# The hybrid decoder trunk on one core: the recurrence's levels in pairs, two to a visit and to a PSUM bank, and two of ScalarE's copies placed later

## Chip, cores and metric

The kernel runs on one core of one Trainium2 chip. The metric is device time in microseconds for one execution of the whole program; the kernel before took 2767.3 us, the median of 3 runs (2766.99 to 2767.32).

TensorE (PE in the rows), VectorE (DVE), ScalarE (ACT) and GpSimd (POOL) each work through a list of their own in order. The list of SyncE (SP) issues the DMAs. Semaphores tie the lists together.

## What is computed

One inference step of a two-layer decoder trunk, for 2048 prompt tokens and 64 sample tokens (8 sequences of 8). Each layer has a projection, two parallel branches (windowed attention and a gated linear recurrence), an output projection with a layer norm, and a gate. The change concerns the recurrence alone. The reference computes it with four heads of 128 x 128 state:

```python
lbf = lb.astype(jnp.float32)
log_f = jnp.logaddexp(jnp.log(lbf), jnp.log1p(-lbf) + jax.nn.log_sigmoid(f_logit.astype(jnp.float32)))
k = -jnp.expm1(log_f)
...
def step(S, blk):
    qc, gc, kc, vc = blk
    G = jnp.cumsum(gc, axis=1)
    diff = G[:, :, None] - G[:, None, :]
    decay = jnp.exp(jnp.where(causal, diff, NEG_INF))
    A = jnp.einsum('bthd,bshd,btshd->bhts', qc, kc, decay)
    o = jnp.einsum('bhts,bshv->bthv', A, vc) + jnp.einsum('bthd,bhdv->bthv', qc * jnp.exp(G), S)
    G_last = G[:, -1]
    S_new = jnp.exp(G_last)[..., None] * S + jnp.einsum(
        'bshd,bshv->bhdv', kc * jnp.exp(G_last[:, None] - G), vc)
    return S_new, o
```

The output o is normed per head, multiplied by a SiLU gate, and goes with the attention's output into the output projection.

## The kernel before

**Phases.** For each of the two layers the program has an attention phase, a recurrence phase (`recurrence_phase`) and an output phase. The recurrence goes over NT = 17 tiles of 128 tokens: tile 0 holds the 64 sample tokens, tiles 1 to 16 the prompt. The order on every engine is written out by hand.

**The matrix A by levels.** Within a tile, A[s, t] for s < t is made in seven levels, h = 64, 32, 16, 8, 4, 2, 1 (`LEVELS`; the text calls them level 0 to level 6), and a diagonal. At level h the tile is cut into blocks of 2h tokens; the second half of each block is multiplied with the first half, both scaled by the exponential of the decay's distance from the middle of the block. The stations of a level are:

1. VectorE, `sub_level` (L1520, L1521): differences of G from the block's middle into `E[l % 2]`. It waits for `level_prod` of two levels before, since E is double buffered.
2. ScalarE, in `middle` (L1366): the exponential of E in place.
3. GpSimd, `level` (L1262): two multiplications, q by E into `qE[l % 2]` and k by E into `kE[l % 2]`, called the factors here. It waits for `level_mm` of two levels before.
4. TensorE, `level` (L1703 for h of 64 and 32, L1707 for the others): 8 or 16 small matmuls with 32 columns of weights into the PSUM bank `LV[l % 2]`. Each shows in the trace as two records.
5. VectorE, `take_level` (L1530, L1538): from the bank into A or into `near`, the 32 x 32 blocks on the diagonal.

**What TensorE does beside it.** In `step(n, k)` TensorE projects the next tile's q, f, g and v (`project`, products at L121 through `split_products`: three per chunk of 128 input rows, 8 chunks, 512 columns each). The levels of tile n are strewn between chunks of that projection: level 0 after chunks 0 and 1 of f, level 1 after 2 and 3, and so on; level 6 stands right before the diagonal (L1715). Between them stand the turning of u (`transpose_u`, L1689, of the tile before) and of q and f of the next tile (`transpose_qf`, L1681 and L1683), which need ScalarE's help: `copy_uT` (L1406) brings u^T out of PSUM for its store by SP, and `copy_z` (L1331) brings q and f out, so that they can be turned. In eight steps of a layer, tiles 3 to 10, `add_sample` (L1750) and `new_dec` (L1615) also update one sample sequence's state, with bank `LV[1]`. A step ends with the turning of kh, the output O and the state's update in M (L1723, L1733, L1734, L1739).

**ScalarE's order in a step.** `middle` does the seven exponentials. `copy_uT` follows the fourth (`if l == (6 if ... else 3)`), then `copy_z(n + 1)` (`if l == 3` in `after`); `split_high` of the next input follows the second. Behind the seventh come the exponentials of the ends (L1377 to L1380), for which GpSimd waits, and then `front_log`, which needs the next tile's g (`z_g`) and starts the next tile's decay.

**The last tile.** While tile 16 goes through its levels, TensorE already does the first products of the output phase (`lead.mix(pe, n, c)`: block n, chunk c, six products). `mix` waits for the low part of the weights' chunk, which VectorE makes (`following.remainder`, L215), one chunk after each `sub_level`; ScalarE rounds the chunks between its exponentials. In step 15, ScalarE and GpSimd split the two blocks of mixT (`lead.split_high`, L313, and `lead.split_low`, L318), which SP loads behind `store_mix`.

## Time and profile before

| | before |
| --- | --- |
| median of 3 runs | 2767.3 us |
| profiled execution | 2765.99 us |
| its span | 2764.2 us, granted clock 0.98 |
| TensorE busy | 2668.4 us, 97% |
| VectorE busy | 1511.1 us, 55% |
| ScalarE busy | 1048.3 us, 38% |
| GpSimd busy | 1044.2 us, 38% |
| recurrence's steps, layer 0 | from about 440 to about 907 us |
| recurrence's steps, layer 1 | end at about 2289 us |

The span is the time between the first and the last instruction of the profiled execution. Matmuls overlap in the trace, so the start of one to the start of the next is what one costs, not its duration. In the chain of waits the pieces follow each other without overlap, so they can be added.

### The profile page before, as it was taken

The page shows a single profiled execution, that of the slowest core. Times are in us where ns is not written, and L with a number is a line of the kernel's source. Part 1 is how long each engine was busy: PE and PEld are TensorE (multiplying, and loading weights), DVE is VectorE, ACT ScalarE, POOL GpSimd, SP SyncE. Part 2 cuts the span into 40 slices and gives each one's busy share as a digit, 9 for nine tenths or more (in the row PEclk, how much of TensorE's full clock was granted, in tenths as well). Part 3 has the DMA queues.
Part 4 walks back from the last instruction along what each step waited for, and adds up shares of the span by engine and source line. Part 5 has one row for each costly group of instructions (what it writes and reads, how often), then busy time and mean ns, then how long its engine had stood idle before and what let it go on. Part 6 is the DMA issues. An engine that isn't in the chain of part 4 may idle for free.

```text
span 2764.2 us, 54510 instructions
## 1 busy us (share of the span) xinstructions
PE 2668.4 (97%) x21010; PEld 2152.0 (78%) x21010; DVE 1511.1 (55%) x3052; ACT 1048.3 (38%) x2305; POOL 1044.2 (38%) x959
## 2 busy tenths in 40 slices
PE   7999989999999799999989999899999997999998
PEld 6777768788877678888777777687888776788887
DVE  5566665677766732222336666656777667322222
ACT  3333354555555521111233333545555555111111
POOL 2222214555555533233212222145555555333332
PEclk9999999999999899999999999989999998999999
...
DMA packets 103450, 190.75 MB, mean 69 GB/s; under 512 B 11744, under 2 KB 64992, under 8 KB 101216
## 3 DMA queue, kind: packets, MB, share of 16 engines
...
q8 instruction: 112, 1.84, 0.3%
q14 instruction: 42, 0.34, 0.0%
q10 hardware_dynamic: 432, 0.08, 0.0%
...
## 4 chain that ended last, share of the span: by engine, by line
PE 90%; issue 3%; DVE 2%; POOL 2%; ACT 1%; DMA 1%; SPq 1%; DVEq 0%; POOLq 0%; ACTq 0%
PE r_Z L121 25%; PE a_Z L121 16%; PE o_GT L2142 13%; PE o_MX L2142 12%; PE o_PL L2142 3%; PE r_LV L1707 2%; PE a_T L977 2%; PE a_SC L956 2%; PE r_LV L1703 1%; PE o_HT L2166 1%; PE a_SC L966 1%; PE r_O L1733 1%; PE r_M L1739 1%; PE r_O L1734 1%; PE o_MX L121 1%
## 5 line engine op out<-in xcount | busy, mean ns | idle before, releaser
L121 PE MATMUL r_Z<-w_rec_high,w_rec_xh 128*128 128x512 f32 x1024 | 433.3, 423 | 1.5 <-DVE r_kT L1484 0.9
L121 PE MATMUL r_Z<-w_rec_high,w_rec_xl 128*128 128x512 f32 x1024 | 403.4, 394 | 0.0
L121 PE MATMUL r_Z<-w_rec_low,w_rec_xh 128*128 128x512 f32 x1024 | 402.7, 393 | 0.0
L121 PE MATMUL a_Z<-w_attn_high,w_attn_xh 128*128 128x512 f32 (+1 forms) x816 | 304.8, 374 | 15.3 <-DVE w_attn_low L213 12.9
L121 PE MATMUL a_Z<-w_attn_high,w_attn_xl 128*128 128x512 f32 (+1 forms) x816 | 292.2, 358 | 0.0
L121 PE MATMUL a_Z<-w_attn_low,w_attn_xh 128*128 128x512 f32 (+1 forms) x816 | 292.0, 358 | 0.0
L1262 POOL TENSOR_TENSOR r_qE<-r_qT,r_E 128x256 f32<-128x256 f32 x230 | 190.5, 828 | 265.4 <-ACT r_E L1366 249.6
L1366 ACT ACTIVATE r_E<-r_E 128x512 f32<-128x512 f32 x230 | 141.5, 630 | 250.3 <-DVE r_E L1521 250.3
L121 PEld LDWEIGHTS r_Z<-w_rec_high,w_rec_xl 128*128 128x128 f32 x1024 | 193.6, 189 | 43.2
L121 PEld LDWEIGHTS r_Z<-w_rec_high,w_rec_xh 128*128 128x128 f32 x1024 | 193.5, 189 | 42.0 <-issue 2.9
L121 PEld LDWEIGHTS r_Z<-w_rec_low,w_rec_xh 128*128 128x128 f32 x1024 | 194.3, 190 | 30.6
L2142 PE MATMUL o_GT<-w_out_high,o_hh 128*128 128x512 f32 x512 | 202.6, 396 | 5.9 <-issue 5.9
L1520 DVE TENSOR_TENSOR r_E<-r_G 128x256 f32<-128x256 f32 x230 | 141.8, 617 | 113.1 <-POOL r_kE L1262 98.2
L2097 DVE SCALAR_TENSOR_TENSOR o_th<-o_th,o_PL 128x1024 f32<-128x1024 f32 x34 | 41.5, 1222 | 296.3 <-PE o_PL L2142 296.3
L2142 PE MATMUL o_MX<-w_out_high,o_mh 128*128 128x512 f32 x480 | 191.4, 399 | 11.4 <-POOL o_ml L1944 11.4
L2142 PE MATMUL o_GT<-w_out_high,o_hl 128*128 128x512 f32 x512 | 201.1, 393 | 0.0
L2142 PE MATMUL o_GT<-w_out_low,o_hh 128*128 128x512 f32 x512 | 201.0, 393 | 0.0
L1262 POOL TENSOR_TENSOR r_kE<-r_kT,r_E 128x256 f32<-128x256 f32 x230 | 200.2, 870 | 0.0
L121 PEld LDWEIGHTS a_Z<-w_attn_high,w_attn_xh 128*128 128x128 f32 x816 | 156.2, 191 | 43.3 <-issue 21.2
L2142 PE MATMUL o_MX<-w_out_low,o_mh 128*128 128x512 f32 x480 | 188.6, 393 | 0.0
L2142 PE MATMUL o_MX<-w_out_high,o_ml 128*128 128x512 f32 x480 | 188.5, 393 | 0.0
L2010 ACT ACTIVATE o_th<-o_GT 128x1024 f32<-128x1024 f32 x34 | 35.0, 1029 | 396.5 <-PE o_GT L2142 376.0
...
## 6 DMA issues: line engine op xcount, KB each, us to landing
...
```

Of the source, the lines that this page charges most:

```text
L121: mm = pe.matmul(out, a[:, c, :], b[:, c, :], start=(first and c == chunks[0] and a is xh and b is wh), stop=(last and c == chunks[-1] and ...
L956: mm = pe.matmul(scores[r:r + 64, 4 * s + i, r:r + 192], qT[rows, i, r:r + 64], keys[:, first_key + r:first_key + r + 192], start=True, st ...
L966: t = pe.transpose(turned[:, h, :], probs[:, h, :], C["ident"][:, :])
L977: mm = pe.matmul(T[d, :], v[tile][:, d], pT[:, i, 4 * s:4 * s + 4, :].rearrange("p h t -> p (h t)"), start=(i == 0), stop=(i == 1))
L1262: op = pool.tensor_tensor(to, halves(flat(q_or_k), h)[half], halves(E[i][:, :], h)[half], ALU.mult)
L1366: act.activation(E[l % 2][:, :], E[l % 2][:, :], ACT.Exp).then_inc(S["level_exp"].sem, 1)
L1520: dve.tensor_tensor(to1, mid, first, ALU.subtract)
L1703: mm = pe.matmul(LV[i][r:r + NEAR, g * h:g * h + h], kE[i][:, g * P + r:g * P + r + NEAR], qE[i][:, g, q], start=True, stop=True)
L1707: mm = pe.matmul(LV[i][r:r + NEAR, g * 16:g * 16 + 16], kE[i][:, g * P + r:g * P + r + NEAR], qE[i][:, g, r // 2:r // 2 + 16], start=True, ...
L2010: act.activation(th[:, :], GT[:, :], ACT.Tanh, scale=0.5).then_inc(S["tanh_done"].sem, 1)
L2097: dve.scalar_tensor_tensor(out=th[:, :], in0=th[:, :], scalar=1.0, in1=PL[:, :], op0=ALU.add, op1=ALU.mult).then_inc(S["blend"].sem, 1)
L2142: mm = pe.matmul(out[0][:, out[1]], a[:, c, :], w, start=(c == 0 and a is high and b is wh), stop=(c == chunks - 1 and a is low))
```

## The change

**Pairs.** Levels 2p and 2p + 1 now go into one bank, `LV[p % 2]`, side by side: the odd one starts at column 256 (`level_bank`). TensorE does both without a projection product between them, and waits for `level_took` only ahead of the even one. So a step has the visits (0, 1), (2, 3), (4, 5) and 6 with the diagonal, where before it had 0, 1, 2, 3, 4, 5 and 6 with the diagonal. The chunks of the projection are dealt out anew between them.

**VectorE** takes two levels after the differences of the odd level that follows: 0 and 1 after those of level 3, 2 and 3 after those of level 5; 4, 5 and 6 after the kh differences. It waits for the products of the whole pair (`visited`). In tile 1, `gated(0, ...)` moves from after level 4 to after level 5.

**ScalarE** does `copy_uT(n - 1)` and `copy_z(n + 1)` behind the sixth exponential (l = 5), no longer behind the fourth. In step 15 the second `lead.split_high` moves from behind the fifth to behind the seventh.

**The last tile**: `lead.mix(pe, 0, 0)` comes ahead of level 0, and the mixes are dealt out in fours between the pairs. In tile 0, the turning of q and f comes ahead of level 0.

The core of the diff:

```diff
@@ -1160,6 +1160,10 @@
         def tokens(n):
 
             return DEC if first(n) else P
+
+        def level_bank(l):
+
+            return LV[l // 2 % 2][:, l % 2 * 256:l % 2 * 256 + 256]
 
         def passed(n):
 
@@ -1364,7 +1368,7 @@
                 for l, h in enumerate(levels):
                     act.wait_ge(*S["level_sub"].at(passed(n) + l + 1))
                     act.activation(E[l % 2][:, :], E[l % 2][:, :], ACT.Exp).then_inc(S["level_exp"].sem, 1)
-                    if l == (6 if isinstance(n, int) and n == 1 else 3):
+                    if l == (6 if isinstance(n, int) and n == 1 else 5):
                         copy_uT(n - 1)
                     after(l)
                 act.wait_ge(*S["khx_done"].at(n + 1))
@@ -1434,13 +1438,13 @@
                 def after(l):
                     if l == 1 and last:
                         lead.split_high(act, 0)
-                    elif l == 4 and last:
+                    elif l == 6 and last:
                         lead.split_high(act, 1)
                     elif l == 1:
                         split_high(n + 2, k)
                     if l == 2 and isinstance(n, int) and n == 1:
                         squares(0, M, DEC)
-                    if l == 3:
+                    if l == 5:
                         copy_z(n + 1)
 
                 middle(n, LEVELS, after)
@@ -1520,12 +1524,12 @@
                 dve.tensor_tensor(to1, mid, first, ALU.subtract)
                 dve.tensor_tensor(to2, second, mid, ALU.subtract).then_inc(S["level_sub"].sem, 1)
 
-            def take_level(n, l, h):
-
-
-                src = LV[l % 2]
+            def take_level(n, l, h, visited):
+
+
+                src = level_bank(l)
                 if h >= NEAR:
-                    dve.wait_ge(*S["level_mm"].at(passed(n) + l + 1))
+                    dve.wait_ge(*S["level_mm"].at(passed(n) + visited))
                     for r in range(0, P, 2 * h):
                         op = dve.tensor_copy(A[r:r + h, :, r + h:r + 2 * h],
                                              src[r:r + h, 0:GH * h].rearrange("p (g t) -> p g t", g=GH))
@@ -1534,7 +1538,7 @@
                         .unsqueeze(1).to_broadcast([P, GH, NEAR // (2 * h), h])
                     if l:
                         dve.wait_ge(*S["level_took"].at(passed(n) + l))
-                    wait_apart(dve, S["dve_passed"], S["level_mm"], passed(n) + l + 1)
+                    wait_apart(dve, S["dve_passed"], S["level_mm"], passed(n) + visited)
                     op = dve.copy_predicated(near[:, :, :].rearrange("p g (n s t) -> p g n s t", s=2, t=h)[:, :, :, 1, :], mask,
                                              src[:, 0:GH * NEAR // 2].rearrange("p (g n t) -> p g n t", g=GH, t=h))
                 op.then_inc(S["level_took"].sem, 1)
@@ -1551,12 +1555,13 @@
                 dve.wait_ge(*S["sum_done"].at(n + 1))
                 if sample is not None:
                     sample_rows(sample)
+                NLEV = len(levels)
                 for l, h in enumerate(levels):
                     sub_level(n, l, h)
                     after(l)
                     if l == 0 and not first(n):
                         silu(n, k)
-                    if l == 4 and second:
+                    if l == 5 and second:
                         gated(0, 0, M, DEC)
                     elif l == 1 and not first(n) and not second:
                         new_state(n - 1)
@@ -1567,8 +1572,9 @@
                         dve.wait_ge(*S["oT_ps"].at(1))
                     elif l == 0:
                         wait(dve, S["o_done"], n)
-                    if l >= 2:
-                        take_level(n, l - 2, levels[l - 2])
+                    if l >= 3 and l % 2:
+                        for taken in (l - 3, l - 2):
+                            take_level(n, taken, levels[taken], l - 1)
                 if first(n):
                     g8 = G[:, :, 0:DEC].rearrange("p g (b t) -> p g b t", t=DEC_SEQ)
                     for g in range(GH):
@@ -1581,8 +1587,8 @@
                     wait(dve, S["khT_ps"], n)
                     dve.tensor_tensor(kh[:, :, :], G[:, :, P - 1:P].to_broadcast([P, GH, P]), G[:, :, :],
                                       ALU.subtract).then_inc(S["khx_done"].sem, 1)
-                for l in (len(levels) - 2, len(levels) - 1):
-                    take_level(n, l, levels[l])
+                for l in range(NLEV - 3 if NLEV > 3 else 0, NLEV):
+                    take_level(n, l, levels[l], min(l // 2 * 2 + 2, NLEV))
                 take_near(n, levels)
 
             def new_state(n):
@@ -1690,21 +1696,22 @@
                 t.then_inc(S["uT_ps"].sem, 1)
 
             def level(n, l, h, sample=None):
-                i, at = l % 2, passed(n) + l
+                i, at, to = l % 2, passed(n) + l, level_bank(l)
                 if sample is not None:
                     pe.wait_ge(*S["sd_done"].at(sample + 1))
                 pe.wait_ge(*S["level_prod"].at(at + 1))
-                wait(pe, S["level_took"], at - (1 if l else 0))
+                if l % 2 == 0:
+                    wait(pe, S["level_took"], at - (2 if l else 0))
                 for g in range(GH):
                     if h >= NEAR:
                         for r in range(0, P, NEAR):
                             block, q = r // (2 * h), slice(r // (2 * h) * h, r // (2 * h) * h + h)
                             if r % (2 * h) < h:
-                                mm = pe.matmul(LV[i][r:r + NEAR, g * h:g * h + h],
+                                mm = pe.matmul(to[r:r + NEAR, g * h:g * h + h],
                                                kE[i][:, g * P + r:g * P + r + NEAR], qE[i][:, g, q], start=True, stop=True)
                     else:
                         for r in range(0, P, NEAR):
-                            mm = pe.matmul(LV[i][r:r + NEAR, g * 16:g * 16 + 16], kE[i][:, g * P + r:g * P + r + NEAR],
+                            mm = pe.matmul(to[r:r + NEAR, g * 16:g * 16 + 16], kE[i][:, g * P + r:g * P + r + NEAR],
                                            qE[i][:, g, r // 2:r // 2 + 16], start=True, stop=True)
                 mm.then_inc(S["level_mm"].sem, 1)
 
@@ -1758,28 +1765,27 @@
                     add_sample(n, sample)
                 if second:
                     turn_samples()
-                project(*later, "f", 0, 2)
+                project(*later, "f", 0, 4)
                 level(n, 0, LEVELS[0])
-                project(*later, "f", 2, 4)
-                level(n, 1, LEVELS[1], sample)
-                project(*later, "f", 4, 6)
+                level(n, 1, LEVELS[1])
+                project(*later, "f", 4, KC)
+                project(*later, "g", 0, 2)
                 if not second:
                     transpose_u(n - 1)
-                level(n, 2, LEVELS[2])
-                project(*later, "f", 6, KC)
+                level(n, 2, LEVELS[2], sample)
                 level(n, 3, LEVELS[3])
-                project(*later, "g", 0, 2)
+                project(*later, "g", 2, 4)
                 transpose_qf(n + 1)
-                project(*later, "g", 2, 4)
-                level(n, 4, LEVELS[4])
                 project(*later, "g", 4, 6)
                 if second:
                     transpose_u(0)
+                level(n, 4, LEVELS[4])
                 level(n, 5, LEVELS[5])
                 project(*later, "g", 6, KC)
+                project(*later, "v", 0, 2)
                 level(n, 6, LEVELS[6])
                 diagonal(n)
-                project(*later, "v")
+                project(*later, "v", 2, KC)
                 transpose_kh(n)
                 if second:
                     pe.wait_ge(*S["zeroed"].at(2))
@@ -1810,11 +1816,10 @@
 
             for what in "qfg":
                 project(1, 1, what)
+            transpose_qf(1)
             level(0, 0, DEC_LEVELS[0])
-            transpose_qf(1)
-            project(1, 1, "v", 0, 2)
             level(0, 1, DEC_LEVELS[1])
-            project(1, 1, "v", 2, 4)
+            project(1, 1, "v", 0, 4)
             level(0, 2, DEC_LEVELS[2])
             diagonal(0)
             project(1, 1, "v", 4, 6)
@@ -1837,19 +1842,24 @@
                 step(2 * j, 0)
             n = NT - 1
             step(n - 1, 1)
-            level(n, 0, LEVELS[0])
             pe.wait_ge(*S["qT_sb"].at(NT))
             pe.wait_ge(*S["kx_done"].at(NT))
             lead.mix(pe, 0, 0)
+            level(n, 0, LEVELS[0])
             level(n, 1, LEVELS[1])
             transpose_u(n - 1)
             pe.wait_ge(*S["gate_done"].at(NT))
             pe.wait_ge(*S["v_copied"].at(NT))
             lead.mix(pe, 1, 0)
-            for l in range(2, NL):
-                lead.mix(pe, 0, l - 1)
+            lead.mix(pe, 0, 1)
+            lead.mix(pe, 1, 1)
+            for l in (2, 4):
                 level(n, l, LEVELS[l])
-                lead.mix(pe, 1, l - 1)
+                level(n, l + 1, LEVELS[l + 1])
+                for c in (l, l + 1):
+                    lead.mix(pe, 0, c)
+                    lead.mix(pe, 1, c)
+            level(n, 6, LEVELS[6])
             diagonal(n)
             lead.mix(pe, 0, NL - 1)
             transpose_kh(n)
```

**What stands where.** TensorE in a step of layer 0, from the turning of u on; r0_qE0 and r0_qE1 are the two factor buffers, even and odd levels. Before:

```order
L1689 MATMUL r0_M<-ident,r0_u 128x128 x4
L1707 MATMUL r0_LV0<-r0_qE0,r0_kE0 32x16 x16
L121 MATMUL r0_Z<-w_rec_high,w_rec_xh1 128x512
L121 MATMUL r0_Z<-w_rec_low,w_rec_xh1 128x512
L121 MATMUL r0_Z<-w_rec_high,w_rec_xl1 128x512
...
L1707 MATMUL r0_LV1<-r0_qE1,r0_kE1 32x16 x16
```

In the changed kernel, from the same point to the turning of q and f:

```order
L1695 MATMUL r0_M<-ident,r0_u 128x128 x4
L1714 MATMUL r0_LV1<-r0_qE0,r0_kE0 32x16 x16
L1714 MATMUL r0_LV1<-r0_qE1,r0_kE1 32x16 x16
L121 MATMUL r0_Z<-w_rec_high,w_rec_xh1 128x512
L121 MATMUL r0_Z<-w_rec_low,w_rec_xh1 128x512
L121 MATMUL r0_Z<-w_rec_high,w_rec_xl1 128x512
...
L1687 MATMUL r0_Z<-ident,r0_zqf 128x128 x4
L1689 MATMUL r0_Z<-ident,r0_zqf 128x128 x4
```

Levels 2 and 3 stand together, in bank LV1, and the six projection products that parted them now stand behind both.

ScalarE in the same kind of step, from the third exponential to the exponentials of the ends (E0 and E1 are the even and odd levels' buffers; zqf is the copy of q and f, r0_u<-r0_M that of u^T). Before:

```order
L1366 ACTIVATE r0_E0<-r0_E0 128x512
L1366 ACTIVATE r0_E1<-r0_E1 128x512
L1406 ACTIVATE r0_u<-r0_M 128x512
L1331 ACTIVATE r0_zqf<-r0_Z 128x1024
L1366 ACTIVATE r0_E0<-r0_E0 128x512
L1366 ACTIVATE r0_E1<-r0_E1 128x512
L1366 ACTIVATE r0_E0<-r0_E0 128x512
L1377 ACTIVATE r0_decay<-r0_G 128x4
L1379 ACTIVATE r0_kh<-r0_kh 128x512
L1380 ACTIVATE r0_qG<-r0_G 128x512
```

In the changed kernel:

```order
L1370 ACTIVATE r0_E0<-r0_E0 128x512
L1370 ACTIVATE r0_E1<-r0_E1 128x512
L1370 ACTIVATE r0_E0<-r0_E0 128x512
L1370 ACTIVATE r0_E1<-r0_E1 128x512
L1410 ACTIVATE r0_u<-r0_M 128x512
L1335 ACTIVATE r0_zqf<-r0_Z 128x1024
L1370 ACTIVATE r0_E0<-r0_E0 128x512
L1381 ACTIVATE r0_decay<-r0_G 128x4
L1383 ACTIVATE r0_kh<-r0_kh 128x512
L1384 ACTIVATE r0_qG<-r0_G 128x512
```

The two copies moved behind two more exponentials, so that six stand ahead of them and one behind.

TensorE at the start of the last tile, from the state's update on (o0_MX and o0_HT take the mix of blocks 0 and 1). Before:

```order
L1739 MATMUL r0_M<-r0_v,r0_khT 128x128 x4
L1703 MATMUL r0_LV0<-r0_qE0,r0_kE0 32x64 x8
L121 MATMUL o0_MX<-w_out_high0,o0_mh0 128x512
L121 MATMUL o0_MX<-w_out_low0,o0_mh0 128x512
L121 MATMUL o0_MX<-w_out_high0,o0_ml0 128x512
...
L1703 MATMUL r0_LV1<-r0_qE1,r0_kE1 32x32 x8
L1689 MATMUL r0_M<-ident,r0_u 128x128 x4
L121 MATMUL o0_HT<-w_out_high0,w_rec_xh1 128x512
```

In the changed kernel:

```order
L1746 MATMUL r0_M<-r0_v,r0_khT 128x128 x4
L121 MATMUL o0_MX<-w_out_high0,o0_mh0 128x512
L121 MATMUL o0_MX<-w_out_low0,o0_mh0 128x512
L121 MATMUL o0_MX<-w_out_high0,o0_ml0 128x512
...
L1710 MATMUL r0_LV0<-r0_qE0,r0_kE0 32x64 x8
L1710 MATMUL r0_LV0<-r0_qE1,r0_kE1 32x32 x8
L1695 MATMUL r0_M<-ident,r0_u 128x128 x4
L121 MATMUL o0_HT<-w_out_high0,w_rec_xh1 128x512
```

The first mix products moved ahead of level 0, and levels 0 and 1 stand together.

## Rows read from the trace of the kernel before

**Rows 1.** The page, chain that ended last: shares of the span by engine.

```profile
PE 90%; issue 3%; DVE 2%; POOL 2%; ACT 1%; DMA 1%; SPq 1%; DVEq 0%; POOLq 0%; ACTq 0%
```

**Rows 2.** Chain in order of time, one step: start us, us, what.

```profile
813.59 6.83 PE r_Z L121 x30
820.42 0.57 PE r_LV L1703 x16
820.99 1.58 PE r_Z L121 x6
...
828.90 0.44 PE r_Z L1681 x4
```

**Rows 3.** Timeline of PE, two visits: start us, us, instruction, xcount.

```profile
580.44 0.39 PE L121 MATMUL r_Z<-w_rec_high,w_rec_xl 128*128 128x512 f32 x1
580.75 0.45 PE L1707 MATMUL r_LV<-r_qE,r_kE 128*32 128x16 f32 x32
581.13 0.50 PE L121 MATMUL r_Z<-w_rec_high,w_rec_xh 128*128 128x512 f32 x1
581.47 0.39 PE L121 MATMUL r_Z<-w_rec_low,w_rec_xh 128*128 128x512 f32 x1
...
582.39 0.40 PE L121 MATMUL r_Z<-w_rec_high,w_rec_xl 128*128 128x512 f32 x1
582.72 0.45 PE L1707 MATMUL r_LV<-r_qE,r_kE 128*32 128x16 f32 x32
582.99 0.47 PE L1715 MATMUL r_M<-r_qT,r_kT 128*32 128x32 f32 x32
...
583.74 0.40 PE L121 MATMUL r_Z<-w_rec_low,w_rec_xh 128*128 128x512 f32 x1
```

**Rows 4.** Timelines of DVE, ACT and POOL in the step from 813.59; idle in brackets.

```profile
825.48 0.95 DVE L1521 TENSOR_TENSOR r_E<-r_G 128x256 f32<-128x256 f32 x1
...
826.93 0.42 DVE L1521 TENSOR_TENSOR r_E<-r_G 128x256 f32<-128x256 f32 x1
...
825.00 0.60 ACT L1406 ACTIVATE r_u<-r_M 128x512 f32<-128x512 f32 x1 [1.06 <-PE r_M L1689]
...
826.98 1.03 ACT L1331 ACTIVATE r_zqf<-r_Z 128x1024 f32<-128x1024 f32 x1 [1.38 <-PE r_Z L121]
...
827.90 1.14 ACT L1366 ACTIVATE r_E<-r_E 128x512 f32<-128x512 f32 x2
...
825.22 0.93 POOL L1262 TENSOR_TENSOR r_kE<-r_kT,r_E 128x256 f32<-128x256 f32 x1
```

**Rows 5.** Chain in order of time, a step with a sample's update.

```profile
560.37 5.49 PE r_Z L121 x24
565.86 0.89 PE r_LV L1750 x8
```

**Rows 6.** Timeline of DVE in that step.

```profile
573.45 0.95 DVE L1521 TENSOR_TENSOR r_E<-r_G 128x256 f32<-128x256 f32 x1
```

**Rows 7.** Timelines in tile 0, in step 15 and in the last tile.

```profile
411.13 0.21 DVE L1538 COPY_PREDICATED r_near<-near,r_LV 128x64 f32<-128x64 int32 x1
...
911.21 1.29 DVE L215 SCALAR_TENSOR_TENSOR w_out_low<-w_out_whole,gains,w_out_high 128x1024 fp32r<-128x1024 f32 x1 [0.70 <-ACT w_out_high L203]
...
891.97 1.06 ACT L313 ACTIVATE w_rec_xh<-w_rec_raw 128x1024 fp32r<-128x1024 f32 x1 [1.52 <-DMA w_rec_raw<-dram_mixT]
...
918.06 0.73 POOL L1262 TENSOR_TENSOR r_kE<-r_kT,r_E 128x256 f32<-128x256 f32 x1
...
895.78 0.44 PE L1707 MATMUL r_LV<-r_qE,r_kE 128*32 128x16 f32 x32 [0.75 <-POOL r_kE L1262]
...
916.48 1.07 PE L1703 MATMUL r_LV<-r_qE,r_kE 128*32 128x64 f32 x16 [9.20 <-POOL r_kE L1262]
```

**Rows 8.** Windows: stretch, length, busy time of each engine, PEclk, DMA share, GB/s.

```profile
916.00:918.00 2.00, 1.52 (x17) 1.33 (x18) 2.00 (x4) 1.54 (x2) 1.84 (x2) 0.50 1.05 410
922.00:924.00 2.00, 2.00 (x11) 1.58 (x9) 2.00 (x4) 0.71 (x2) 1.22 (x2) 1.00 0.03 8
```

## The prediction

> **What bounds the kernel now.** I read the shares of the chain that ended last first [rows 1]: 90% of the span is TensorE work, and no other engine or queue holds more than 2%. Then the chain in order of time through one step of the recurrence, the one that starts at 813.59 [rows 2]: there it is TensorE alone, piece after piece with nothing between, so in a step every nanosecond that TensorE saves is saved, as long as nobody makes it wait. There are 15 such steps in each of the two layers, 30 in all. Below, "+x" is the time after a step's start. Last I read TensorE's own timeline around two visits to the levels [rows 3]. Projection products of 512 columns start every 0.23 us (581.47 to 582.39 are four). The sixth level's visit (580.75) costs more than its own products: from the projection product at 580.44 to the one at 581.47 there are 1.03 us where two products take 0.46, so a visit costs 0.57. Of that about 0.08 goes on entering (0.31 instead of 0.23 to the first small product) and 0.11 on the product after the return (0.34 instead of 0.23), the rest is the 0.38 of the visit, whose last 0.11 is a tail: in the next visit the level's products hand over to those of the diagonal after 0.27 (582.72 to 582.99).
>
> **Two levels a visit.** That next visit is the experiment that I need, already in the trace: level 6 and diagonal side by side. From 582.39 to 583.74 are 1.35, less 0.46 is 0.89, so the second set of small products added 0.32 where a visit of its own costs 0.57. It has 32 columns; a level of 16 columns should add only the 0.27 until handover. So a merge saves 0.25 at least and 0.30 if the handover row holds for it; an upper bound is 0.32 (entry 0.10 as at 582.39 to 582.72, tail 0.11, return 0.11). I take 0.30, since the second sets in this change are levels, which is the row for the same shapes. A step goes from seven visits to four (levels 0 and 1; 2 and 3; 4 and 5; 6 with the diagonal as now), so three merges: 0.90 a step, 27.0 over 30 steps, bounds 22.5 and 28.8. The number of products, their shapes and banks' total use stay as they are.
>
> What the rows show is that leaving the wide products for the 32-column ones and coming back costs some 0.2 to 0.3 us each time. The Trainium skill, TensorEngine Tiling, Key Properties, says that changing the tiling mode drains TensorE, while changing only the tile doesn't; by that rule the saving is the whole price of a switch, and it holds for level 0 with its 64 columns too. The trace bears it out for level 6 and the diagonal; no row here shows it for two levels.
>
> **What the waits of the merged visits cost.** A merged visit needs the factors of both levels. Level 0's visit now starts at +6.83 [rows 2] and moves behind two more chunks of f: 6 products, 1.38, so +8.2. Then come both levels (0.57 - 0.11 + 0.38 = 0.84), 18 projection products (the six right after a visit take 1.58, the other twelve 2.77) and the turning of u (as long as that of q at 828.90, 0.44): levels 2 and 3 at about +13.9. GpSimd's factors of level 3 end at 825.22 + 0.93, +12.6 [rows 4], and nothing ahead of them moves later: 1.3 to spare. So this wait costs nothing. The last pair has what it needs earlier still, because ScalarE no longer stops between the exponentials: now it waits 1.38 there for f (826.98 in [rows 4]).
>
> **What is moved behind the third pair, and where it is tight.** TensorE turns q and f (now at 828.90, +15.3) right after two chunks of g. By the sum above that comes to +13.9 + 0.65 + 1.6 = +16.1. It needs ScalarE's copy of q and f, and that copy now stands behind the sixth exponential and the copy of u^T. The chain to it [rows 4]: VectorE's differences for level 4 end at 825.48 + 0.95, +12.8. Those for level 5 need the factors of level 3 (+12.6), so they follow at once; if GpSimd stands still meanwhile they take 0.76, as the pair that ends with 826.93 does: +13.6. And it does stand still, for its factors of level 4 need level 2's product, at +14.2 or later. Then the exponential of level 5 (0.57), the copy of u^T (0.60, of which ScalarE overlaps about 0.1 with the next) and the copy of q and f (1.03): about +15.7. That leaves 0.3 us, and the copy of u^T finds its input, turned at +13.4 to +13.9, just ready. The eight steps of a layer that also update a sample's state have less. Such a step starts at 560.37 and has 0.89 more on TensorE before level 0 [rows 5], which puts the turn of q and f at +17.0. The differences of level 4 end at 573.45 + 0.95, which is +14.0 [rows 6], so the copy ends at about +16.9. There it is a tie, and I take 0.1 for 15 or so of the 30 steps: 1.5 lost. Bounds: none lost, or 0.2 in each step, 6.0. SP's store of u^T and the load behind it move later by some 2.7 us. They have over 10 us until the next gated u needs the buffer, so no price.
>
> **The edges.** (a) In tile 0, VectorE no longer takes a level (0.21, 411.13 in [rows 7]) ahead of the differences that ScalarE's chain waits for: 0.15 a layer, 0.3. (b) In step 15 of each layer ScalarE splits the second block of mixT; now it waits for its load, 1.52, in layer 0 (891.97 in [rows 7]), and TensorE with it. That load is queued on SP behind the store of u^T, which moves later, and the split moves behind the seventh exponential, with the exponentials of the ends and the logarithm for the last tile queued behind it on ScalarE. I put 0.9 on this wait. In layer 0 it takes the place of the 0.75 that TensorE loses now (row 895.78), so it costs nothing there; in layer 1, where little is lost now, it costs 0.9. Bounds: 0 and 2.4 (0.9 + 1.52). (c) In the last tile TensorE waits 9.20 us for GpSimd (916.48 in [rows 7]); after it the clock is at half [rows 8], and the first six mix products run at it, 2.8 us by twice the spacing of [rows 3]. They need only chunk 0's low part, which VectorE has at 911.21 + 1.29. The change puts them first, so they go into the wait. But level 1 must wait until 918.06 + 0.73 for its factors, and from there VectorE's splitting of the weights paces the levels. I take a gain of 0.4 a layer, 0.8; bounds are a gain of 1.1 each and a loss of 2.1 each (below).
>
> **The sum.** 27.0 - 1.5 + 0.3 - 0.9 + 0.8 = 25.7. The profiled execution took 2765.99 us (span 2764.2), which gives 2740.3. It stands 1.3 under the median of the three runs shown, 2767.3, and against that I forecast 2741.6.
>
> **The rivals.** First, the clock in the last tile. Its granted clock is 0.50 in 916 to 918 and back at 1.00 by 922 to 924, after unbroken work from 916.48 [rows 8]. Changed, TensorE works on six products from 912.5, stops, does level 0, stops for level 1 and again for u. If these stops keep it at 1.2 GHz, the next 18 mix products take 8.3 instead of 4.1 us. They start about 1.1 earlier than now, and a wait of about 1 for level 3's factors hides some of it: about 2.1 lost per layer instead of 0.4 gained, some 5 us over both, 2746.6. The Trainium skill, TensorE: Matmul & The Clock Gate, Why this matters for your kernels, asks for continuous work before the full clock comes back, and so speaks against this part of the change; rows 8 agree that unbroken work brings it back. Chance 0.09.
>
> Second, the merges save nothing: the price would lie in each level's own hand-over and not in the switch. Then only the edges remain and the tie at q and f costs 1.5: 2767 to 2769. The visit with the diagonal in [rows 3] speaks against it. Chance 0.04. Third, the copy of q and f comes late by a full 1.1 in every step, because VectorE's level-5 differences run while GpSimd works: 0.95 and more for each instead of 0.42, as the row at 825.48 has it beside 825.22. That gives back the 0.90, about 2766. What speaks against it is that GpSimd must wait for level 2's product. Chance 0.04. The Trainium skill, SBUF — State Buffer, section SBUF: two separate sides, calls the shared port an exclusive lock for the whole instruction; the rows show both sides stretched, 0.95 and 0.93, which is the same direction.
>
> Fourth, and slower: the same place, but with level 4's differences late as well, since level 2's factors wait for a level-0 product that is now 1.4 later (+8.2). Then the two delays of 1.1 add up, the turn of q and f stalls about 2.0 beyond its slack, and each step is 1.1 longer: 33 us, 2800. It decides when the copy of q and f ends more than 1.2 us after the +15.7 worked out. Against it: level 2's exponential ends at about +9.4, after level 0's product even when moved. Chance 0.03. That the change doesn't do what it says I don't hold a case of its own: the order has the levels in pairs in all 30 steps.
>
> **How the numbers follow.** Forecast 2741.6, chance 0.80, own range 2735 to 2751. The range for 8 in 10 takes in the bounds: all at their best 28.8 + 0.3 + 2.2 = 31.3, 2736, with 2 us for what one execution leaves open, 2734; and on the other side 22.5 - 6.0 + 0.3 - 0.9 - 2 = 13.9, 2753.4, so 2754. The clock rival lies in it. A difference of 0.2% (5.5 us) is about what a measurement of this kernel can tell from none. Faster by more than that: the forecast and the first rival, 0.89. Within it: the second and third, 0.08. Slower: 0.03.
>
> **What would show it.** In the changed profile a step without a sample should take 30.0 to 30.1 us on TensorE, with about 0.27 from the first to the second set of a pair and 0.38 for the second. TensorE should wait nowhere but, if anywhere, for ScalarE's copy of q and f, 0.1 at most. The factors of level 3 should end 1 us or more before their visit, and the two differences of level 5 should take about 0.42 each. ScalarE should have no wait for f between its exponentials. In the last tile the first mix products should start at about 912.5 less what was saved before, with the clock as above. I am wrong if a wait for q and f of 0.5 or more stands in most steps, if a pair costs what two visits did, or if the last tile grows by more than 2 us.

## The result and the profile after

The changed kernel takes 2739.86 us (median of 4 runs, 2738.89 to 2740.91); the kernel before took 2767.31 in the same comparison. The ratio is 0.9906, with a 95% interval of 0.9893 to 0.992: 27.45 us, or 1.0%, faster. The profiled execution took 2740.13 us (span 2738.3), 25.86 less than that of before. The forecast was 2741.6.

The page of the changed kernel has TensorE's busy time 24.0 us lower than before, and the shares of the chain that ended last, beside [rows 1], are still nearly all TensorE:

```profile
PE 2644.4 (97%) x21010; PEld 2158.7 (79%) x21010; DVE 1514.6 (55%) x3052; ACT 1048.6 (38%) x2305; POOL 1038.6 (38%) x959
```

```profile
PE 90%; DVE 3%; ACT 2%; issue 2%; DMA 1%; POOL 1%; SPq 1%; DVEq 0%; POOLq 0%; ACTq 0%
```

The chain of waits through one step without a sample, in the place of [rows 2] (start us, us, what):

```profile
770.39 8.19 PE r_Z L121 x36
778.57 0.81 PE r_LV L1710 x29
779.39 4.31 PE r_Z L121 x18
783.70 0.44 PE r_M L1695 x4
784.13 0.67 PE r_LV L1714 x52
784.80 1.59 PE r_Z L121 x6
786.39 0.44 PE r_Z L1687 x4
...
788.67 0.67 PE r_LV L1714 x52
789.34 2.94 PE r_Z L121 x12
792.28 0.38 PE r_LV L1714 x32
...
800.40 0.69 PE r_Z L121 x3
```

Nothing stands between TensorE's pieces. The step takes 800.40 - 770.39 = 30.01 us. A pair of levels costs 0.67 (with level 0 in it 0.81), where two visits to levels of 16 columns cost 0.38 each and 0.20 more for the return to the wide products after each (1.59 for six of them instead of 1.38 to 1.41).

The rest of the comparison is one table. It is worked out from VectorE's timeline: the time from its first product of kT in one tile (L1484 before, L1488 after) to the same in the next. That cuts the recurrence into stretches of one tile each, in layer 0 / layer 1. The last row goes from there to the last update product of tile 16 (L1739 before, L1746 after). "Before, again" is the first experiment below.

| stretch | before | before, again | after | gained | forecast |
| --- | --- | --- | --- | --- | --- |
| tile 0 | 20.18 / 20.18 | 20.18 / 20.18 | 20.03 / 20.04 | 0.29 | 0.3 |
| tile 1 | 43.30 / 44.95 | 46.54 / 46.59 | 42.83 / 46.04 | -0.62 | 1.8 |
| steps 2 to 14 | 409.97 / 409.89 | 410.14 / 409.92 | 397.69 / 397.57 | 24.60 | 21.9 |
| step 15 | 31.68 / 30.85 | 31.74 / 32.00 | 29.97 / 30.74 | 1.82 | 0.9 |
| last tile | 42.67 / 42.76 | 42.94 / 42.87 | 42.00 / 43.34 | 0.09 | 0.8 |
| outside the recurrence | | | | -0.32 | 0 |
| sum | | | | 25.86 | 25.7 |

The total fits better than its parts do, and the rows of tile 1 and of the last tile, from one execution each, are mostly chance, as the experiments show. The 1.5 us that the forecast took off for the tie at the copy of q and f are counted with steps 2 to 14.

### The profile page after: what moved, and what is told of

Read it like the earlier page. It is cut to its first block, busy times and chain, and to the rows that moved or that the text cites. A ratio compares the mean times of both kernels' runs of the same rounds, so it can differ in the third digit from the quotient of the medians.

```text
span 2738.3 us, 54412 instructions
## 1 busy us (share of the span) xinstructions
PE 2644.4 (97%) x21010; PEld 2158.7 (79%) x21010; DVE 1514.6 (55%) x3052; ACT 1048.6 (38%) x2305; POOL 1038.6 (38%) x959
## 4 chain that ended last, share of the span: by engine, by line
PE 90%; DVE 3%; ACT 2%; issue 2%; DMA 1%; POOL 1%; SPq 1%; DVEq 0%; POOLq 0%; ACTq 0%
PE r_Z L121 25%; PE a_Z L121 16%; PE o_GT L2152 13%; PE o_MX L2152 12%; PE o_PL L2152 3%; PE a_T L977 2%; PE r_LV L1714 2%; PE a_SC L956 2%; PE o_HT L2176 1%; PE r_M L1746 1%; PE r_O L1741 1%; PE r_O L1740 1%; PE a_SC L966 1%; PE r_Z L259 1%; PE r_LV L1710 1%
## 5 line engine op out<-in xcount | busy, mean ns | idle before, releaser
L121 PE MATMUL r_Z<-w_rec_high,w_rec_xh 128*128 128x512 f32 x1024 | 423.4, 414 | 1.5 <-DVE r_kT L1488 0.9
L121 PEld LDWEIGHTS r_Z<-w_rec_high,w_rec_xl 128*128 128x128 f32 x1024 | 193.8, 189 | 42.7
L121 PEld LDWEIGHTS r_Z<-w_rec_high,w_rec_xh 128*128 128x128 f32 x1024 | 193.9, 189 | 41.2 <-issue 2.9
L121 PEld LDWEIGHTS a_Z<-w_attn_high,w_attn_xl 128*128 128x128 f32 x816 | 155.6, 191 | 23.9
```

Of the source, the lines that this page charges most:

```text
L121: mm = pe.matmul(out, a[:, c, :], b[:, c, :], start=(first and c == chunks[0] and a is xh and b is wh), stop=(last and c == chunks[-1] and ...
```

## The experiments

**The kernel before, once more.** No edit.

> The kernel before, once more, as it is. Between the two traces shown, stretches that the change doesn't touch differ too: 0.8 us in the attention of layer 1 and 2.5 us between the layers. If those are chance from one execution to the next, this trace moves by as much against the first trace of before in the same places; if the change causes them in a way not seen, it reproduces the first trace within 0.3 us there. Its steps should take 30.95 us and, with a sample, 31.89 in either case.

Measured: 2772.7 us. Its steps take 30.95 to 30.99 us and 31.86 to 31.90 with a sample, as before. But tile 1 takes 46.54 and 46.59 us where the first trace has 43.30 and 44.95, and step 15 of layer 1 takes 32.00 instead of 30.85. So these two stretches change by up to 3.3 and 1.2 us with no change at all, and the rows "tile 1" and "step 15" of the table, read alone, say nothing on the change. Outside the recurrence it moves too. The first product of kT in layer 0 starts at 396.44 instead of 397.22 (the changed kernel: 395.04), and from layer 0's last update product to the first kT of layer 1 it has 834.4 us instead of 833.6. The changed kernel has 836.0 there, which is more than this one run shows; but the other kernels of this study, with the same code in that place, have 833.0 to 835.4.

**One merge undone.** In `step`:

```diff
                 level(n, 4, LEVELS[4])
-                level(n, 5, LEVELS[5])
                 project(*later, "g", 6, KC)
+                level(n, 5, LEVELS[5])
                 project(*later, "v", 0, 2)
```

> The changed kernel with one merge undone: level 5 stands two chunks of g behind level 4, everything else stays. Theory: each merge saves the price of leaving the wide products and coming back, 0.31 us, so a step without a sample takes 30.33 us instead of 30.02, a sample step 31.29 instead of 30.98, and 30 steps cost 9.3 us: 2749.2. Rival, the gain lies in ScalarE's order and the merges only fill the time: a step stays at 30.02 and the total at 2740.

Measured: 2745.43 us (2744.09 to 2747.24), ratio to before 0.993 (0.9911 to 0.9949). Steps take 30.30 us and 31.21 with a sample; steps 2 to 14 take 401.24 in each layer where the changed kernel has 397.63 on average: 3.61 / 13 = 0.28 for each merge. Its chain shows where (start us, us, what):

```profile
789.47 0.38 PE r_LV L1714 x32
789.85 1.59 PE r_Z L121 x6
791.43 0.38 PE r_LV L1714 x32
791.81 1.59 PE r_Z L121 x6
```

These 3.94 us stand where the changed kernel has 0.67 + 2.94 = 3.61, and the six products ahead take 0.04 less. The price lies in the merge, and ScalarE's order, which is the same in both, doesn't supply it. The total is 5.6 us over the changed kernel's, not the 9.3 expected and not the 8.4 that 30 steps at 0.28 make: tile 1 takes 40.92 and 45.75 us in this trace, 2.2 less than in that of the changed kernel. So the price is read from the steps, which agree from one to the next, and not from the total.

**All three merges undone**, with the banks, the waits, VectorE's takes and ScalarE's copies left as the change has them:

```diff
                 level(n, 0, LEVELS[0])
+                project(*later, "f", 4, 6)
                 level(n, 1, LEVELS[1])
-                project(*later, "f", 4, KC)
+                project(*later, "f", 6, KC)
...
                 level(n, 2, LEVELS[2], sample)
-                level(n, 3, LEVELS[3])
                 project(*later, "g", 2, 4)
+                level(n, 3, LEVELS[3])
```

(and level 5 as above.)

> The changed kernel with all three merges of a step undone (level 1 behind chunks 4 and 5 of f, level 3 behind chunks 2 and 3 of g, level 5 behind chunks 6 and 7 of g); ScalarE's copies, the banks and VectorE's takes stay as in the changed kernel. Theory: three times 0.31, a step takes 30.95 us, as before the change, and the total is 2740 + 28 = 2768. Rival, part of the gain is ScalarE's no longer stopping between the exponentials or the fewer waits of VectorE: a step stays well under 30.95, by as much as that part is worth, and the total is under 2760.

Measured: 2763.58 us (2760.12 to 2767.49 in 10 runs), ratio 0.999 (0.9979 to 1.0001), so no longer to be told from before. Steps take 30.91 and 31.83 us, steps 2 to 14 409.29 in each layer: (409.29 - 397.63) / 13 = 0.90 for the three merges. A step gained 0.946, so this kernel keeps 0.05 over the one before. A likely place, argued and not tested, is level 3, which stands here right ahead of the turning of q and f: TensorE returns to wide work there at a price of 0.59 - 0.44 = 0.15 instead of 0.20. In the changed kernel no level stands there, so if this is the place, undoing the merges gives back 0.05 less than they are worth, and the whole 0.946 is theirs. By the pieces of the two chains, levels 0 and 1 give 0.36, levels 2 and 3 0.23 with that 0.05 missing, levels 4 and 5 0.31.

```profile
799.27 0.38 PE r_LV L1714 x32
799.65 0.59 PE r_Z L1687 x4
```

**The diagonal parted from level 6**, a set of 32-column products that isn't a level:

```diff
+                diagonal(n)
                 project(*later, "v", 0, 2)
                 level(n, 6, LEVELS[6])
-                diagonal(n)
```

> The changed kernel with the opposite of a merge where before already had one: the diagonal's 32-column products stand two chunks of v ahead of level 6 instead of right behind it; the last tile stays as it is. Theory, the price belongs to the switch, whatever set of 32-column products is parted: 0.31 us a step, 30.33 without a sample, 30 steps cost 9.3 us, total 2749. Rival, the price belongs to a level's own hand-over (its wait on GpSimd's factors and its bank), which the diagonal doesn't have: under 0.1 us a step, total 2740 to 2743.

Measured: 2743.73 us (2743.32 to 2747.95), ratio 0.9921 (0.9902 to 0.9939). Steps take 30.26 to 30.32 us, steps 2 to 14 401.14: 3.51 / 13 = 0.27 a step. The total is only 3.9 us over the changed kernel's, where the steps say 8.1 and 9.3 was expected; the reading rests on the steps again. The chain (start us, us, what):

```profile
798.61 0.39 PE r_M L1722 x32
799.00 1.59 PE r_Z L121 x6
800.59 0.38 PE r_LV L1714 x32
```

The diagonal alone costs 0.39 plus 0.2 on the products behind it, like a level. So the price is that of leaving the wide products and coming back, for both kinds of 32-column products that this kernel has. That refutes the rival "a level's own hand-over", in a place that the change doesn't touch. The Trainium skill (TensorEngine Tiling, Key Properties) says that TensorE drains when the tiling mode changes and not when the tile alone does. This case agrees: an excursion costs 0.27 to 0.30 us, and a second set of 32-column products beside the first doesn't pay it again. That it is a drain, no row shows.

**ScalarE's copies back behind the second pair**, all else as changed:

```diff
-                    if l == (6 if isinstance(n, int) and n == 1 else 5):
+                    if l == (6 if isinstance(n, int) and n == 1 else 3):
                         copy_uT(n - 1)
...
-                    if l == 5:
+                    if l == 3:
                         copy_z(n + 1)
```

> The changed kernel with ScalarE's two copies (u^T, then q and f) behind the second pair's exponentials again, as before the change. Theory, the move is what lets the merged visit of levels 4 and 5 find its factors: both exponentials of that pair then wait until the copies are done, about 2.5 us later than the 783.12 of the changed trace, GpSimd's factors of level 5 are ready at +18.8 instead of +17.5, and the visit, due at +18.28, waits 0.5 to 0.6 us in every step: a step takes 30.5 to 30.6 us, 30 steps cost 15 to 18 us, total 2755 to 2758. Rival, the move isn't needed, since the factors had slack: a step stays at 30.02. Rival, the whole gain is the move: a step takes 30.95.

Measured: 2754.88 us (2750.74 to 2759.07), ratio 0.9959 (0.9946 to 0.9972). Steps take 30.65 to 30.68 us, a little over the 30.5 to 30.6 expected: 0.64 more than changed, 16.6 over the 26 steps 2 to 14. Timelines of this kernel, PE in one step, ACT and POOL in the next, 30.66 later (idle before, and for whom, in brackets):

```profile
799.18 0.45 PE L1714 MATMUL r_LV<-r_qE,r_kE 128*32 128x16 f32 x32
800.12 0.45 PE L1714 MATMUL r_LV<-r_qE,r_kE 128*32 128x16 f32 x32 [0.50 <-POOL r_kE L1266]
...
825.41 0.60 ACT L1410 ACTIVATE r_u<-r_M 128x512 f32<-128x512 f32 x1 [3.75 <-PE r_M L1695]
825.90 1.02 ACT L1335 ACTIVATE r_zqf<-r_Z 128x1024 f32<-128x1024 f32 x1
826.81 1.15 ACT L1370 ACTIVATE r_E<-r_E 128x512 f32<-128x512 f32 x2
...
829.71 1.02 POOL L1266 TENSOR_TENSOR r_kE<-r_kT,r_E 128x256 f32<-128x256 f32 x1
```

ScalarE stands 3.75 us for the turned u, the third pair's exponentials come behind the copies, and level 5's factors end at 830.73, when level 4's product has already been done: TensorE stands 0.50 us between the two levels of one visit. Without the move of the copies two thirds of what the merges save is lost.

**The copies moved in the kernel before**, without merges:

```diff
-                    if l == (6 if isinstance(n, int) and n == 1 else 3):
+                    if l == (6 if isinstance(n, int) and n == 1 else 5):
                         copy_uT(n - 1)
...
-                    elif l == 4 and last:
+                    elif l == 6 and last:
...
-                    if l == 3:
+                    if l == 5:
                         copy_z(n + 1)
```

> The kernel before with ScalarE's two copies moved behind the third pair's exponentials and nothing merged (the split of the second mixT block in step 15 stands behind the seventh exponential, as in the change). Theory: nothing is gained, and the turn of q and f, which stands earlier there than in the changed order (+15.3 instead of +16.0), waits 0.2 to 0.4 us for the copy: a step takes 31.2 to 31.3, total 2773 to 2779. Rival, the gain of the change is the move: a step takes 30.0 to 30.5.

Measured: 2785.46 us (2781.93 to 2792.89), ratio 1.008 (1.0055 to 1.0104): slower, and twice as much as expected. A step takes 31.50 us, with a sample 32.18 or 32.96. Timelines of PE, one step without and one with a sample, and of ACT ahead of the first:

```profile
802.05 0.40 PE L121 MATMUL r_Z<-w_rec_high,w_rec_xl 128*128 128x512 f32 x1
802.77 0.66 PE L1681 MATMUL r_Z<-ident,r_zqf 128*128 128x128 f32 x4 [0.33 <-ACT r_zqf L1331]
803.27 0.60 PE L1683 MATMUL r_Z<-ident,r_zqf 128*128 128x128 f32 x4
...
544.20 0.66 PE L1681 MATMUL r_Z<-ident,r_zqf 128*128 128x128 f32 x4 [0.82 <-ACT r_zqf L1331]
...
801.71 1.02 ACT L1331 ACTIVATE r_zqf<-r_Z 128x1024 f32<-128x1024 f32 x1
```

The wait of 0.33 is what the expectation had, and the step loses 0.55. The rest is how idle time is counted. A projection product takes 0.40 in the trace, but without a stop the turning starts 0.23 after it; the idle time is counted only from its end, so it leaves out the first 0.16. From start to start, the turning of q comes 0.72 after the last product instead of 0.23 (0.49 lost), and that of f 0.50 after it instead of 0.44 (0.06 lost): 0.55 together. In the same way a sample step with the wait of 0.82 loses 1.04. The sample steps of 32.18 lose 0.29, with the turning 0.2 us late and no idle time shown at all.

So each half of the change needs the other: merged without the move, two thirds of the gain go into a wait at levels 4 and 5; moved without the merges, a wait at the turning of q and f makes it slower.

**Level 0 first in the last tile**, all else as changed:

```diff
             step(n - 1, 1)
+            level(n, 0, LEVELS[0])
             pe.wait_ge(*S["qT_sb"].at(NT))
             pe.wait_ge(*S["kx_done"].at(NT))
             lead.mix(pe, 0, 0)
-            level(n, 0, LEVELS[0])
             level(n, 1, LEVELS[1])
```

> The changed kernel with level 0 of the last tile ahead of the first six mix products again, as before the change. From VectorE's first write of kT for the last tile to the last tile's update products the changed trace has 42.0 us in layer 0 and 43.3 in layer 1, the two traces of before 42.7 to 42.9 in both. Theory, the six products in the wait are worth 0.4 to 0.7 a layer and the 1.3 between the layers is when the clock comes back: 42.5 to 42.9 in at least one layer, none under 42.3. Rival, the stops after the six products are what keeps the clock at half in layer 1: with level 0 first both layers take 42.0 or less.

Measured: 2737.82 us in one run. The last tile takes 42.55 us in layer 0 and 41.97 in layer 1, 84.5 together, where the changed kernel has 42.00 + 43.34 = 85.3. Neither expectation holds: one layer is over 42.3, the other under it. With one execution of each, 0.8 us is no verdict. The traces with one or all merges undone, the diagonal parted and the sample states spread have the last tile as the changed kernel has it, so there are ten such tiles: 42.00 to 43.39 us, 42.5 on average, beside 42.7 to 42.9 (42.8 on average) in the four of before. The two of this kernel lie among them. What can be read is the clock. In layer 1 of the changed kernel, TensorE stops three times after the six products, and the clock is still at half in 2278 to 2280; in this kernel it works unbroken from 2270.31, and the clock is back in the window from 2274 to 2276. Timeline of PE and windows (stretch, length, busy time of each engine, PEclk, DMA share, GB/s), first changed, then this one:

```profile
2272.07 1.07 PE L1710 MATMUL r_LV<-r_qE,r_kE 128*32 128x64 f32 x16 [0.97 <-POOL r_kE L1266]
2274.41 0.64 PE L1710 MATMUL r_LV<-r_qE,r_kE 128*32 128x32 f32 x16 [1.27 <-POOL r_kE L1266]
2275.51 1.11 PE L1695 MATMUL r_M<-ident,r_u 128*128 128x128 f32 x4 [0.46 <-DVE r_u L1609]
```

```profile
2278.00:2280.00 2.00, 2.00 (x6) 1.52 (x6) 2.00 (x3) 0.89 (x2) 0.97 (x2) 0.50 0.00 0
```

```profile
2270.31 1.06 PE L1710 MATMUL r_LV<-r_qE,r_kE 128*32 128x64 f32 x16 [9.74 <-POOL r_kE L1266]
```

```profile
2274.00:2276.00 2.00, 2.00 (x25) 1.65 (x25) 2.00 (x4) 1.60 (x2) 0.89 (x1) 0.82 0.06 25
```

**Two moves at the edge.** In the changed kernel GpSimd has its factors of level 0 in the last tile only after a root and a split of 3.37 us, all of them behind step 15's output (timeline of POOL, layer 1), though it had stood idle before:

```profile
2266.91 3.37 POOL L318 TENSOR_TENSOR w_rec_xl<-w_rec_raw,w_rec_xh 128x1024 fp32r<-128x1024 f32 x1
2270.24 0.91 POOL L1266 TENSOR_TENSOR r_qE<-r_qT,r_E 128x256 f32<-128x256 f32 x1
```

```diff
-            root(NT - 2)
             lead.split_low(pool, 1)
+            root(NT - 2)
...
-                    elif l == 6 and last:
-                        lead.split_high(act, 1)
...
                 copy_khT(n)
+                if last:
+                    lead.split_high(act, 1)
                 front_exp(n + 1)
```

> The changed kernel with two moves at its edge. (1) In step 15 ScalarE splits the second mixT block behind its copy of kh^T, where it stands idle, instead of behind the seventh exponential. Theory, what step 15 takes over a plain step (30.74 instead of 30.02 in layer 1 of the changed trace, 31.6 and 31.7 in others) is ScalarE waiting for that block's load: 30.1 us at most in both layers, whenever the load comes. Rival, it is a load's contention or the clock: 30.7 stays. (2) GpSimd takes the low part of that block before the root of the last but one tile, where it is idle for 7 us, instead of behind it, so its factors of level 0 in the last tile start 3.0 us earlier. Theory: the last tile is 1 to 2 us shorter a layer; rival, VectorE's splitting of the weights sets the pace there: under 0.5 us.

Measured: 2731.58 us (2730.24 to 2733.5), ratio 0.9874 (0.9855 to 0.9893). Step 15 takes 29.92 us in both layers, and 29.90 or 29.92 in all the traces below with this move, so what it took over a plain step was ScalarE's wait for the block's load. The other move can't have done it: GpSimd starts that split at 2258.77, when step 15 has ended at 2254.72. The last tile takes 40.86 and 40.14 us, 1.1 and 3.2 less than changed; the eight tiles with both moves average 40.4, 2.1 under the ten without, where 1 to 2 was expected. Layer 1 of this kernel (timelines of POOL and PE):

```profile
2258.77 2.35 POOL L318 TENSOR_TENSOR w_rec_xl<-w_rec_raw,w_rec_xh 128x1024 fp32r<-128x1024 f32 x1 [3.75 <-ACT w_rec_xh L313]
...
2264.76 0.89 POOL L1266 TENSOR_TENSOR r_qE<-r_qT,r_E 128x256 f32<-128x256 f32 x1 [1.20 <-ACT r_E L1370]
...
2269.39 0.64 PE L1710 MATMUL r_LV<-r_qE,r_kE 128*32 128x32 f32 x16 [0.28 <-POOL r_kE L1266]
```

**Wide products among the sample states' narrow ones.** Tile 1 was left, with its 41 to 46.6 us from one execution to the next. Its clock is at half for 10 to 21 us in all around the 64 products of 8 columns by which tile 0 reads the sample states.

```diff
-            sample_states(0, 4)
+            sample_states(0, 1)
             project(1, 1, "v", 6, KC)
-            sample_states(4, DEC_BATCH)
+            for b in range(1, DEC_BATCH - 1):
+                sample_states(b, b + 1)
+                project(2, 0, "q", b - 1, b)
+            sample_states(DEC_BATCH - 1, DEC_BATCH)
...
-                project(*later, "q")
+                project(*later, "q", DEC_BATCH - 2 if second else 0)
```

> The changed kernel with tile 2's projection of q, which stood behind the sample states' products, one chunk behind each of six of them (three wide products each), chunks 6 and 7 of v behind the first state; the amount of work is the same. It tests why tile 1 takes 41 to 46.6 us from one execution to the next whatever the kernel: its granted clock is at half for 14 to 20 us after the 64 products of 8 columns. Theory, those narrow products take the clock down, and wide ones among them hold it up: tile 1 takes under 40 us and the total is 2730 or less. Rival, the clock falls for another reason (the wait at the end of tile 0, the heavy work before it): tile 1 stays at 41 to 47 and the total at 2740 plus or minus 4.

Measured: 2738.61 us, with the widest range of all, 2725.51 to 2746.44. In the profiled execution tile 1 takes 49.15 and 49.13 us, outside what either side of the expectation had: here the wide products among the narrow ones didn't hold the clock, so the theory fails as a rule. But this execution is the slowest of the four. That of 2725.51 is 20.9 us faster, with a mean granted clock of 0.985 instead of 0.978; by these two means it spent some 39 us less at half clock, an estimate, which is worth those 20 us. If that was in tile 1, it took about 39 us there, as the theory had it; it has no trace. In the trace the granted clock is down from before 418 to after 444 (windows), through all eight states:

```profile
416.00:418.00 2.00, 2.00 (x15) 1.82 (x14) 1.97 (x9) 0.00 (x0) 0.00 (x0) 0.90 0.00 0
418.00:420.00 2.00, 2.00 (x9) 1.71 (x7) 0.68 (x1) 1.25 (x3) 0.00 (x0) 0.50 0.44 131
...
444.00:446.00 2.00, 2.00 (x9) 1.59 (x8) 0.64 (x2) 2.00 (x10) 0.00 (x0) 0.78 0.00 0
```

**The narrow products bunched**, on top of the two edge moves:

```diff
             transpose_kh(0)
+            project(1, 1, "v", 6, KC)
...
-            sample_states(0, 4)
-            project(1, 1, "v", 6, KC)
-            sample_states(4, DEC_BATCH)
+            sample_states(0, DEC_BATCH)
```

> The kernel with both edge moves (step 15's split and GpSimd's low part) and one more: chunks 6 and 7 of v, which stood between the fourth and the fifth sample state, go ahead of the first one, into the wait for ScalarE's gather, so that all 64 products of 8 columns follow each other and unbroken wide work begins behind them. Parting them with wide products made tile 1 longer (49.1 us, 27 us at half clock), so the theory is now that the clock comes back only when wide work runs unbroken: tile 1 takes 39 to 43 us in both layers instead of 41 to 46.6, total 2724 to 2731. Rival, where the clock falls is chance and the order of the narrow products is nothing to it: tile 1 stays at 41 to 46.6 and the total at 2731 plus or minus 3. A third way: the states' loads come late without the wide products between, a wait of 1 to 3 us a layer in front of the fifth state.

Measured: 2727.06 us (2724.92 to 2728.38), ratio 0.9857 (0.9836 to 0.9879); tile 1 takes 41.00 and 42.19 us. As this kernel and the one with only the edge moves ran on different chips, both were run again side by side:

> The kernel with the two edge moves once more, on the same chip as the next one, since the two were timed on different chips and tile 1's time changes from one execution to the next. If the bunching is worth something, this one keeps tile 1 at 41 to 46.6 us and a total of 2729 to 2734, 2 us or more above the next. If it isn't, both have the same tile 1 and totals within 2 us.

> The kernel with the two edge moves and the sample states' products bunched, once more, beside the one without the bunching. If wide work that runs unbroken brings the clock back sooner: tile 1 at 40 to 43 us in both layers, total 2724 to 2729. If the first look was chance: tile 1 over 43 in one layer at least, total 2729 to 2734.

Measured: 2730.44 us (2728.41 to 2732.05) without the bunching, tile 1 46.05 and 41.23; 2724.36 (2722.4 to 2725.3) with it, ratio to before 0.9844 (0.9827 to 0.986), tile 1 40.76 and 40.66. All four bunched tiles lie between 40.66 and 42.19 (41.2 on average). Eight tiles of kernels that have tile 1 as changed lie between 41.23 and 46.06 (44.0 on average), and the eight in which only step 1's merges, copies or diagonal differ between 40.92 and 46.04. So the bunching takes away the long tiles and leaves the shortest about as short as they were. The bunched kernel's chain and windows:

```profile
417.82 2.79 DMA r_s_dec<-dram_state
...
420.65 6.49 PE r_O L1800 x32
...
427.43 7.67 PE r_Z L121 x24
```

```profile
420.00:422.00 2.00, 1.82 (x14) 1.71 (x13) 1.79 (x5) 1.18 (x3) 0.00 (x0) 0.84 0.91 269
...
430.00:432.00 2.00, 2.00 (x7) 1.53 (x7) 1.61 (x2) 0.17 (x1) 1.92 (x3) 0.60 0.00 0
```

The clock still falls, in the window from 420 to 422, and is back in that from 430 to 432; in the kernel with only the edge moves it comes back in that from 436 to 438 (0.63). The chain now goes through the load of the fifth state, the third way of the expectation; what TensorE loses by it is small, a wait of 0.18 to 0.30 us in the four bunched tiles.

The edit does two things at once. The six products of v also fill a wait for ScalarE's gather (rows of PE, the changed kernel and the bunched one):

```profile
415.55 1.08 PE L1830 MATMUL r_O<-r_A,r_v_dec 128*128 128x64 f32 x8 [0.67 <-ACT r_A L1390]
...
415.94 1.00 PE L1831 MATMUL r_O<-r_A,r_v_dec 128*128 128x64 f32 x8
```

How much each is worth follows from the time at half clock, four times what PEclk lacks to 1 summed over windows of 2 us. It is 10 to 20.5 us in the eight tiles with tile 1 as changed (16.2 on average) and 10.2 to 13.6 in the bunched ones (11.1). Take half of it off, and what is left of the tile is 35.9 us on average and 35.6. So of the 2.9 us that a bunched tile saves, some 2.6 are clock and 0.3 the filled wait (estimates from these windows). What is not shown is the reason that the expectation gave. In layer 1 of the kernel with only the edge moves (41.23 us) the clock is back, at 0.86 and 0.99, in the windows from 1792 to 1796, with the second half of the narrow products in them, and at half again in that from 1796 to 1798: it came back without the long unbroken work behind the last state. The bunched kernel is the fastest of the study, 42 us (1.6%) under the kernel before on the same chip.

## Why the prediction was right, point by point

**The merges.** Forecast: 0.30 for each, 0.90 a step, from the visit of level 6 with the diagonal [rows 3]. Measured by undoing them: 0.90 for the three, 0.28 for levels 4 and 5, 0.27 for level 6 and the diagonal. With the 0.05 that the undone kernel keeps, they may be worth 0.95. The second set of a pair was to start after 0.27 and take 0.38; a pair's 0.67 in the chain is near the sum. The step was to take 30.0 to 30.1 us and takes 30.01.

**The waits of the merged visits.** Levels 2 and 3 were due at +13.9 and come at +13.74. Level 3's factors were due at +12.6 and end at +12.4. Both are in these rows of the step from 770.39 (timelines of POOL, DVE and ACT):

```profile
781.90 0.91 POOL L1266 TENSOR_TENSOR r_kE<-r_kT,r_E 128x256 f32<-128x256 f32 x1
...
783.35 0.41 DVE L1525 TENSOR_TENSOR r_E<-r_G 128x256 f32<-128x256 f32 x1
...
784.34 0.58 ACT L1410 ACTIVATE r_u<-r_M 128x512 f32<-128x512 f32 x1
784.81 1.02 ACT L1335 ACTIVATE r_zqf<-r_Z 128x1024 f32<-128x1024 f32 x1
```

Level 5's differences take 0.41, with GpSimd idle, so the third rival (0.95 and a late copy) didn't occur, and with it not the fourth.

**The tie at q and f: the term that was wrong.** Forecast: copy ready at +15.7 in a plain step and +16.9 with a sample, 1.5 us lost. Measured: the copy ends at 785.83, +15.44, and the turning starts at 786.39, +16.00; with a sample (step from 523.78) the copy ends at 539.38 + 1.02 = 540.40, +16.62, and the turning starts at 540.71, +16.93. The times of TensorE were right to 0.1; the chain of differences, exponentials and copies was put 0.25 too late, and nothing is lost. The room was less than it looks, though, in the forecast too: it set a time of the chain for the turning against times of the timelines for the copy, and the timeline has the turning 0.16 earlier (786.23 and 540.55). By one and the same view 0.40 us was to spare in a plain step and 0.15 with a sample. The run with the copies moved but nothing merged shows that the term was worth having: with TensorE there 0.7 us earlier, the same place costs 0.29 to 1.04 a step.

**Tile 0.** 0.3 forecast, 0.29 measured.

**Tile 1.** It was counted with the other steps, at 0.9 a layer. That was a wrong view of what sets its time: the clock, which was at half for some 14 us of it in the first trace of before (from the window at 422, 0.65, to that at 436, 0.94), and which moves it by over 5 us with the same code. The -0.62 of the table is that chance. With half of the time at half clock taken off, as above, the four tiles of before keep 36.3 to 36.5 us and the eight with tile 1 as changed 35.8 to 36.1: a gain of 0.4 a layer, half of the 0.9 forecast (an estimate from windows).

**Step 15.** The mechanism was the right one, ScalarE's wait for the second block; the chance in it was not seen. Before, ScalarE stood 2.7 us in two waits, by this row of the waits (total us, times, longest); after the change, one of 0.83 was left (timeline of ACT):

```profile
ACT w_rec_xh L313 <- DMA w_rec_raw<-dram_mixT: 2.7, 2, 1.5
```

```profile
2251.33 1.06 ACT L313 ACTIVATE w_rec_xh<-w_rec_raw 128x1024 fp32r<-128x1024 f32 x1 [0.83 <-DMA w_rec_raw<-dram_mixT]
```

The forecast had 0.9 lost in layer 1 and nothing net in layer 0. In layer 0 the load was in time and the step gained 1.71, the 0.95 and the 0.75 of [rows 7]; in layer 1 the 0.83 took away nearly all of it, as forecast. The same stretch moved by 1.15 between the two traces of before, and the moved split fixed it at 29.92.

**The last tile.** 0.4 a layer forecast; 0.67 gained in layer 0, 0.58 lost in layer 1. These two are the shortest and nearly the longest of the ten tiles with this order, whose average is 0.3 under before's, so the term was about right and its two measured values are chance. The first rival, the clock kept at half by the stops, came true in one layer of the two, and cost there 1.0 us against the forecast instead of the 2.5 it was priced at. The changed rows answer to [rows 8]: the clock came back in the window from 904 to 906 (0.65) in layer 0, right behind the turning of u at 903.15, and in that from 2280 to 2282 (0.75) in layer 1, with the turning at 2275.51, though both had the same three stops. The Trainium skill (TensorE: Matmul & The Clock Gate, Why this matters for your kernels) asks for continuous work before the full clock; layer 1 beside the kernel with level 0 first agrees, layer 0 shows that stops alone don't settle it. Nor does the clock wait for the end of the stops: in the trace with the spread states it is back in the window from 905 to 907 (0.83), behind the six products, and down again in that from 909 to 911 (0.53), behind a stop of 1.70 us, and that tile takes 42.15.

What the prediction had right for the right reason is nine tenths of the result, the 0.90 a step. That the sum came within 0.2 us of the profiled difference is luck: the tie that cost nothing (+1.5), the 0.05 a step over the 0.90 (+1.2) and step 15 (+0.9) made up for tile 1 (-2.4), the last tile (-0.7) and the rest (-0.3). The stated range, 2735 to 2751, is narrower than the 2734 to 2754 that the forecast's own bounds gave, and these left out the worst of step 15 (2.4) and of the last tile (4.2), which together would reach 2757.
